# One product and one masked copy per level for both directions of a gated linear attention

## The reference

```python
def _hgrn_chunk_scan(q, k, v, log_f, s0):
    # S_t = diag(f_t) S_{t-1} + k_t outer v_t, o_t = S_t^T q_t, chunkwise
    ...
        b = jnp.cumsum(lf, axis=-2)
        diff = b[..., :, None, :] - b[..., None, :, :]
        decay = jnp.where(causal, jnp.exp(jnp.where(causal, diff, 0.0)), 0.0)
        scores = jnp.einsum('bhtd,bhtsd,bhsd->bhts', qb, decay, kb)
        o = jnp.einsum('bhts,bhsv->bhtv', scores, vb) + jnp.einsum('bhtd,bhdv->bhtv', qb * jnp.exp(b), S)
    ...

def _hgrn_bidir(q, v, lf_f, k_f, lf_b, k_b, s_f, s_b):
    o_f, s_f = _hgrn_chunk_scan(q, k_f, v, lf_f, s_f)
    rev = lambda a: jnp.flip(a, axis=1)
    o_b, s_b = _hgrn_chunk_scan(rev(q), rev(k_b), rev(v), rev(lf_b), s_b)
    return o_f + rev(o_b), s_f, s_b
```

## Time and profile before

| | us |
|---|---|
| median of 3 runs | 4889.44 |
| lowest and highest run | 4884.33, 4891.63 |
| span of the profiled execution | 4883.9 |
| TensorE busy in it | 4403.1 (90%) |
| VectorE busy | 2831.0 (58%) |
| ScalarE busy | 1812.8 (37%) |
| masked copies L1311, 120 of them | 0.735 each (median) |

### The profile page before, as it was taken

One profiled execution on the slowest core, in us unless ns is written; L12 is line 12 of the kernel. 1 busy time (PEld: TensorE's weight loads), 2 busy tenths in 40 slices (PEclk: granted clock), 3 DMA queues, 4 the chain that ended last, 5 costly groups with the idle time before them and its releaser, 6 DMA issues. The chain is left out here.

```text
span 4883.9 us, 59716 instructions
## 1 busy us (share of the span) xinstructions
PE 4403.1 (90%) x22171; PEld 3685.4 (75%) x22171; DVE 2831.0 (58%) x4958; ACT 1812.8 (37%) x2536; POOL 413.0 (8%) x308
## 2 busy tenths in 40 slices
PE   7988888878998566999999996999999999999998
PEld 5877775655874255999999995767878877777887
DVE  0777776674445987888888886334343333444332
ACT  1655654443321033333333333336233233543322
POOL 0000000000002501222222220000000000000000
PEclk9999999998999788999999998999999999999999
DMA  7111111102221025777778873211323322122332
GB/s 263 56 40 36 38 35 43 39 13 79 93 86 53 18 104 229 280 269 278 282 268 278 282 267 107 69 61 48 98 90 98 94 96 65 46 76 91 99 93 84
DMA packets 196095, 579.63 MB, mean 119 GB/s; under 512 B 17344, under 2 KB 66752, under 8 KB 194368
## 3 DMA queue, kind: packets, MB, share of 16 engines
q1 hardware_dynamic: 158032, 435.34, 26.2%
q0 software_dynamic: 36864, 134.23, 8.1%
q10 hardware_dynamic: 1008, 7.49, 0.4%
HBM read 549.73 MB, written 27.26 MB: 118 GB/s over the span
## 5 line engine op out<-in xcount | busy, mean ns | idle before, releaser
L402 DVE TENSOR_TENSOR tile_rest<-tile_raw,tile_up 128x1024 fp32r<-128x1024 f32 (+2 forms) x288 | 338.6, 1180 | 787.7 <-ACT tile_up L393 787.5
L410 PE MATMUL layer_psum<-hn_up,tile_up 128*128 128x512 f32 x1344 | 534.7, 398 | 21.2 <-DVE hn_rest L497 21.2
L411 PE MATMUL layer_psum<-hn_up,tile_rest 128*128 128x512 f32 x1344 | 527.4, 392 | 0.0
L412 PE MATMUL layer_psum<-hn_rest,tile_up 128*128 128x512 f32 x1344 | 527.2, 392 | 0.0
L393 ACT ACTIVATE tile_up<-tile_raw 128x1024 fp32r<-128x1024 f32 (+2 forms) x288 | 291.4, 1017 | 369.6 <-PE layer_psum L412 368.5
L2190 PE MATMUL ex_psum<-ex_t_up,ex_u_up 128*128 128x384 f32 x1024 | 344.0, 336 | 11.3 <-ACT ex_prod L2264 5.9
L2208 PE MATMUL ex_psum<-ex_prod_up,ex_v_up 128*128 128x384 f32 x1024 | 342.8, 335 | 2.8 <-DVE xT L2330 2.8
L2191 PE MATMUL ex_psum<-ex_t_up,ex_u_rest 128*128 128x384 f32 x1024 | 343.7, 336 | 0.0
L2192 PE MATMUL ex_psum<-ex_t_rest,ex_u_up 128*128 128x384 f32 x1024 | 343.6, 336 | 0.0
L2209 PE MATMUL ex_psum<-ex_prod_up,ex_v_rest 128*128 128x384 f32 x1024 | 342.8, 335 | 0.0
L2210 PE MATMUL ex_psum<-ex_prod_rest,ex_v_up 128*128 128x384 f32 x1024 | 342.6, 335 | 0.0
(11 more groups left out here) (448 smaller groups left out, 10119.2 us busy)
## 6 DMA issues: line engine op xcount, KB each, us to landing
ex_u<-in_peer_u SPq DMA_DIRECT2D x128, 512.0 KB, 6.8
tT<-in_peer_v SPq DMA_DIRECT2D x128, 512.0 KB, 7.3
tile_raw<-in_w_gu SPq DMA_DIRECT2D x88, 512.0 KB, 3.5
xT<-in_w_head SPq DMA_DIRECT2D x56, 512.0 KB, 3.6
mod_w<-in_w_ada SPq DMA_DIRECT2D x48, 512.0 KB, 4.8
mg_w_raw<-in_w_merge SPq DMA_DIRECT2D x48, 512.0 KB, 3.6
expert_table<-et_rows SPq DMA_DIRECT2D x6, 4096.0 KB, 11.3
ex_rows<-expert_table SPq DMA_DIRECT2D x64, 384.0 KB, 7.9
```

Of the source, the lines that this page charges most:

```text
L402: self.nc.vector.tensor_tensor(out=self.rest[:, n % self.SLOTS, 0:blocks, :], in0=self.raw[n % self.RAWS][:, 0:blocks, :], in1=self.up[:, ...
L410: self.nc.tensor.matmul(dst, w_up, up, start=first, stop=False)
L411: self.nc.tensor.matmul(dst, w_rest, up, start=False, stop=False)
L412: return self.nc.tensor.matmul(dst, w_up, rest, start=False, stop=last)
```

## The change

For levels 0 to 6 the slots are filled by role instead of by direction: `qk[slot][:, KEYS, :]` takes the scaled keys of both directions, `qk[slot][:, QUERIES, :]` the scaled queries. In each pair of blocks the left half of KEYS holds the forward keys and the right half the backward keys, and QUERIES the other way round, so that a product of a block of KEYS with the same block of QUERIES holds the wanted scores of both directions. There are 4 products a level instead of 8, one copy under one mask instead of two, and 8 masks instead of 15. The multiplications keep their number and form and write to other rows. The score banks still follow in turn, but each level takes one instead of two; the waits for `o_squared` and `o_raw` move to levels 2 and 3, those for `masked` start at level 4, and the products after level 6 use other banks. Levels 7 and 8 are computed as before.

```diff
-N_MASKS = 2 * IN_CHUNK + 1
+N_MASKS = IN_CHUNK + 1
...
+    KEYS, QUERIES = 0, 1
...
+        SCORES = IN_CHUNK + 6
...
-                n = 0
                 for level in range(IN_CHUNK):
                     pe.wait_ge(qk_ready, START + h * (LEVELS + 1) + level + 1)
-                    for dr in range(2):
-                        if n == 2:
-
-                            pe.wait_ge(o_squared, START + h)
-                        elif n == 3:
-                            pe.wait_ge(o_raw, START + h)
-                        elif n >= 4:
-                            pe.wait_ge(masked, START + h * N_MASKS + n - 3)
-                        for b in range(TB):
-                            blk = qk[qk_at(level)][:, dr, b * P:(b + 1) * P]
-                            last = nc.tensor.matmul(score_bank(n)[:, b * P:(b + 1) * P], blk, blk, start=True, stop=True)
-                        last.then_inc(score_filled, 1)
-                        n += 1
+                    if level == 2:
+
+                        pe.wait_ge(o_squared, START + h)
+                    elif level == 3:
+                        pe.wait_ge(o_raw, START + h)
+                    elif level >= 4:
+                        pe.wait_ge(masked, START + h * N_MASKS + level - 3)
+                    for b in range(TB):
+                        s = slice(b * P, (b + 1) * P)
+                        last = nc.tensor.matmul(score_bank(level)[:, s], qk[qk_at(level)][:, KEYS, s],
+                                                qk[qk_at(level)][:, QUERIES, s], start=True, stop=True)
+                    last.then_inc(score_filled, 1)
...
-                pe.wait_ge(masked, START + h * N_MASKS + n - 3)
+                pe.wait_ge(masked, START + h * N_MASKS + 4)
                 for b in range(TB):
                     s = slice(b * P, (b + 1) * P)
-                    last = nc.tensor.matmul(B[4][:, s], ksum[:, s], q[:, s], start=True, stop=True)
+                    last = nc.tensor.matmul(B[5][:, s], ksum[:, s], q[:, s], start=True, stop=True)
...
-                pe.wait_ge(masked, START + h * N_MASKS + 12)
+                pe.wait_ge(masked, START + h * N_MASKS + 5)
...
-                    last = nc.tensor.matmul(B[5][:, at * P:(at + 1) * P], qk[qk_at(7)][:, dr, s * P:(s + 1) * P],
+                    last = nc.tensor.matmul(B[6][:, at * P:(at + 1) * P], qk[qk_at(7)][:, dr, s * P:(s + 1) * P],
...
-                    dve.wait_ge(score_filled, START + h * 20 + n + 1)
+                    dve.wait_ge(score_filled, START + h * SCORES + n + 1)
...
-                    bank = score_bank(n) if n < 2 * IN_CHUNK else B[4]
+                    bank = score_bank(n)
...
-                        dve.wait_ge(score_filled, START + h * 20 + 2 * (level - QK_TURNS) + 2)
+                        dve.wait_ge(score_filled, START + h * SCORES + level - QK_TURNS + 1)
...
                         g = halves(grow[:, level % 2, dr, :], level, T)
-                        out = halves(qk[qk_at(level)][:, dr, :], level, T)
                         for side in range(2):
 
-                            by = q if side == 1 - dr else k[:, dr, 0:T]
+                            of = QUERIES if side == 1 - dr else KEYS
+                            by = q if of == QUERIES else k[:, dr, 0:T]
+                            out = halves(qk[qk_at(level)][:, of if level < IN_CHUNK else dr, :], level, T)
                             ins = nc.vector.tensor_tensor(out=out[:, :, side, :], in0=g[:, :, side, :],
                                                           in1=halves(by, level, T)[:, :, side, :], op=ALU.mult)
...
-                        to_blocks(2 * level - 2)
-                        to_blocks(2 * level - 1)
+                        to_blocks(level - 1)
...
-        masks += [same & left_s & ~left_t, same & ~left_s & left_t]
+        masks.append(same & (left_s != left_t))
```

More of the change, by code:

```diff
@@ L921, in head @@
                 pe.wait_ge(qk_ready, START + h * (LEVELS + 1) + LEVELS)
-                pe.wait_ge(masked, START + h * N_MASKS + 13)
+                pe.wait_ge(masked, START + h * N_MASKS + 6)
                 for b in range(2):
-                    last = nc.tensor.matmul(B[6][:, b * C:(b + 1) * C], qk[qk_at(8)][:, 0, b * P:(b + 1) * P],
+                    last = nc.tensor.matmul(B[7][:, b * C:(b + 1) * C], qk[qk_at(8)][:, 0, b * P:(b + 1) * P],
                                             qk[qk_at(8)][:, 0, C:T], start=True, stop=True)
                 last.then_inc(score_filled, 1)
-                pe.wait_ge(masked, START + h * N_MASKS + 14)
+                pe.wait_ge(masked, START + h * N_MASKS + 7)
                 for b in range(2):
-                    last = nc.tensor.matmul(B[7][:, b * C:(b + 1) * C], qk[qk_at(8)][:, 1, C + b * P:C + (b + 1) * P],
+                    last = nc.tensor.matmul(B[4][:, b * C:(b + 1) * C], qk[qk_at(8)][:, 1, C + b * P:C + (b + 1) * P],
                                             qk[qk_at(8)][:, 1, 0:C], start=True, stop=True)
@@ L940, in head @@
                     for dr in range(2):
-                        last = nc.tensor.matmul(B[4 + b][:], full[:, dr, T + b * P:T + (b + 1) * P], full[:, dr, 0:T],
+                        last = nc.tensor.matmul(B[5 + b][:], full[:, dr, T + b * P:T + (b + 1) * P], full[:, dr, 0:T],
                                                 start=dr == 0, stop=dr == 1)
@@ L1050, in keys @@
                     act.wait_ge(k_read, START + h)
-                    act.wait_ge(score_filled, START + (h - 1) * 20 + 15)
+                    act.wait_ge(score_filled, START + (h - 1) * SCORES + N_MASKS)
                 evacuate(("k0", h), k[:, 0, 0:T], bank_of(("k0", h)))
@@ L1136, in head @@
                     keys(h + 1)
-                act.wait_ge(score_filled, START + h * 20 + 16)
+                act.wait_ge(score_filled, START + h * SCORES + N_MASKS + 1)
                 for at, (s, t) in enumerate(((0, 1), (2, 3), (1, 0), (3, 2))):
-                    nc.scalar.activation(sx[:, s, t * P:(t + 1) * P], B[5][:, at * P:(at + 1) * P],
+                    nc.scalar.activation(sx[:, s, t * P:(t + 1) * P], B[6][:, at * P:(at + 1) * P],
                                          ACT.Copy).then_inc(score_out, 1)
@@ L1142, in head @@
                     magnitudes(h + 1)
-                act.wait_ge(score_filled, START + h * 20 + 17)
-                nc.scalar.activation(sx[:, 0:2, C:T], B[6][:].rearrange("p (b t) -> p b t", b=2),
+                act.wait_ge(score_filled, START + h * SCORES + N_MASKS + 2)
+                nc.scalar.activation(sx[:, 0:2, C:T], B[7][:].rearrange("p (b t) -> p b t", b=2),
                                      ACT.Copy).then_inc(score_out, 1)
-                act.wait_ge(score_filled, START + h * 20 + 18)
-                nc.scalar.activation(sx[:, 2:4, 0:C], B[7][:].rearrange("p (b t) -> p b t", b=2),
+                act.wait_ge(score_filled, START + h * SCORES + N_MASKS + 3)
+                nc.scalar.activation(sx[:, 2:4, 0:C], B[4][:].rearrange("p (b t) -> p b t", b=2),
                                      ACT.Copy).then_inc(score_out, 1)
@@ L1151, in head @@
                 for b in range(CB):
-                    act.wait_ge(score_filled, START + h * 20 + 19 + b)
-                    nc.scalar.activation(sc[:, b, :], B[4 + b][:], ACT.Copy).then_inc(score_out, 1)
+                    act.wait_ge(score_filled, START + h * SCORES + N_MASKS + 4 + b)
+                    nc.scalar.activation(sc[:, b, :], B[5 + b][:], ACT.Copy).then_inc(score_out, 1)
                 if more:
```

## The result

| | before | changed |
|---|---|---|
| median (us) | 4886.89 (4 runs) | 4840.32 (4 runs) |
| lowest and highest run | 4883.86, 4891.63 | 4839.83, 4842.53 |
| ratio, with its 95% interval | | 0.9905, 0.9893 to 0.9917 |
| span of the profiled execution | 4883.9 | 4840.7 |
| TensorE, VectorE, ScalarE busy | 4403.1, 2831.0, 1812.8 | 4356.1, 2788.2, 1813.2 |

The change takes 46.6 us off the median and 43.2 off the span; the forecast was 43.8, and 4845.6 as a median. The total is right. Its parts are less so: the odd heads gave more than forecast, the even heads less, and the first phase a little more.

What follows compares the result with a forecast made beforehand. TensorE's queue was taken to bind odd heads, a mixed chain of TensorE, VectorE and ScalarE even heads. Gains of 29.8 + 12.9 + 1.1 = 43.8 us from 4889.4 gave 4845.6 us, range 4834 to 4862.

Steps and rivals of the forecast that it cites:

- Odd heads bound by TensorE: Heads 0, 1, 3, 5, 7: TensorE's queue has no gap, so halved products save 5.95 us each, 29.8 us.
- half of it is 0.85 us: A level's products take 1.70 us of TensorE's queue; halving them saves 0.85 us, 5.95 us a head.
- It can hardly be more: Odd heads: the gain hardly exceeds 5.95 us each, since TensorE stays full and what follows is untouched.
- Even heads: Heads 2, 4, 6: a mixed chain of TensorE, VectorE and ScalarE gains 4.3 us each, 12.9 us; bounds 2.8 and 5.8.
- this takes TensorE's slow stretch as it is: Even heads, around level 6: the lower clock stays as before; its 1.5 us could vanish or come twice.
- rival B's first case: One more clock fall in each even head costs 4.6 us, giving 4850.2 us, inside the forecast's own range.
- Rival A: Only odd heads gain; ScalarE's table loads and cuts hold even heads: 30.9 us, 4858.5 us; chance 0.12.
- Rival B: TensorE idles more, so its clock falls more often; two more falls in all eight heads, 4870.1 us: chance 0.05.
- Rival C: Slower: clock falls reach the fills; two whole fills per head at the lower level give 4937 us; chance 0.03.
- Rival D: Nothing gained in heads, which end on ScalarE's chain; only the masks' 1.1 us remain, 4888 us; chance 0.04.
- Masks: First phase: seven masks no longer loaded shorten TensorE's wait for a weight tile by 1.1 us; bounds 0 and 1.5.
- Waits and operands: Heads: moved waits for o_squared, o_raw and free banks, and distinct operands of a product, were priced at 0.

Runs made afterwards that it cites:

- e7: Changed kernel, but the mask table keeps the room of 15 masks in SBUF, with 8 loaded and used: 4844.8 us.
- e2: Changed kernel, but each masked copy of levels 0 to 6 is issued twice: 4858.3 us.
- e4: Changed kernel, plus unused products of constants on TensorE before levels 1 and 6 in heads 2, 4 and 6: 4830.2 us, ratio to before 0.9881.
- e3: Changed kernel, but 15 masks are loaded instead of 8, the seven more unused: 4847.5 us.
- e8: Changed kernel, with the queries' fill moved behind level 5 and 10 unused products before level 1 in heads 2, 4 and 6: 4829.3 us.

## Why the prediction was right, and where its terms were off

**Odd heads bound by TensorE (29.8 us): right, and undersized.** Measured: 6.3, 6.3, 6.4, 6.0 and 6.5 us, together 31.6. The step that was mis-sized is "half of it is 0.85 us". The products' place did not halve from 1.70 to 0.85 but went to 0.81, so each level gave 0.89; it is 0.81 in e7 too, where the tiles stand as before. 7 x 0.89 = 6.2. Why half the products take less than half the place, no run shows. "It can hardly be more" was wrong by that much. That VectorE would keep up was right: its level 8 and TensorE's fill arrived together again, and e2 shows what it costs where it does not (1.8 us).

**Even heads (12.9 us): the chain was right, the size was not.** Measured: 2.7, 3.2 and 3.8 us, together 9.7, just below to inside the bounds of 2.8 and 5.8. The step that failed is "this takes TensorE's slow stretch as it is". The longer gaps brought a second fall of the clock in each even head, in the head's end (head 2) or behind level 1 (heads 4 and 6), which was rival B's first case; it should have had the larger chance, since the forecast itself said that both gaps would grow. And in head 2 the fall before level 6 reached further than before. ScalarE's start of the head and TensorE behind level 6, before:

```profile
302.86 1.49 ACT L1097 ACTIVATE hd_k<-hd_k 128x1536 f32<-128x1536 f32 x1
...
347.76 0.48 PE L601 MATMUL mx_psum<-x_up,mx_w_up 128*128 128x512 f32 x1
...
353.42 1.05 PE L917 MATMUL mx_psum<-attT 128*128 128x128 f32 x8
...
358.85 3.67 PE L941 MATMUL mx_psum<-hd_full 128*128 128x512 f32 x8 [2.64 <-DVE convT L1311]
```

And in the changed kernel (the head starts at 287.98):

```profile
328.48 0.77 PE L601 MATMUL mx_psum<-x_up,mx_w_up 128*128 128x512 f32 x1
...
334.90 1.05 PE L918 MATMUL mx_psum<-attT 128*128 128x128 f32 x8
...
340.32 5.37 PE L942 MATMUL mx_psum<-hd_full 128*128 128x512 f32 x8 [2.64 <-DVE convT L1312]
```

Up to level 6 the working came out: its products stand 37.07 us behind the head's start instead of 40.81 (343.67), 3.7 us sooner where 3.45 were worked out. From there to L918 it takes 9.85 us where it took 9.75, although one halved product had to make it 0.85 shorter: the clock was already low when the gap ended, and the fourth fill took 6.42 us instead of 5.66. The fall in the head's end then stretched L942 from 3.67 to 5.37 us, of which 0.95 came through to the next products.

e4 shows the size of the falls. Heads 4 and 6, free of them, are 6.4 and 6.9 us shorter than before; head 2, with the one in its end left, 5.2. These gains include the fall that each head had before the change, so they answer to the upper bound of 5.8 and not to the 4.3. They pass even that, since heads 4 and 6 of before were 69.3 and 69.7 us long and not 69.0 like head 2, the one that the working read.

**Rival A** fell: even heads did gain. **Rival B**'s sign was met: a clock below 1 in stretches where it was 1 before was on the prediction's own list of what would show it wrong, and here it stands in the even heads and in head 1. **Rival C** did not come: the falls lengthened one fill of an even head by up to 1.8 us (7.3 instead of 5.5). **Rival D** fell with the first head.

**Masks (1.1 us): the size fits, the cause is not settled.** The first phase's products end 1.5 us sooner, and e3 gives 1.3 for the load; but e4, with the small load, ends as late as e3, and part of the difference is a fall of the clock that the prediction did not have. The heads begin 2.2 us sooner; the 0.7 us between goes with a shorter slow stretch of the clock in the first fills (e3, which ends the phase 1.3 us later, begins its heads 1.9 us later).

**Waits and operands (0): right.** No new idle time stands before a level's products in odd heads, and L910's products kept their 0.81 us.

**What lies around the span.** "5.5 us below the median, outside the span and unchanged" was wrong. The changed kernel's profiled run has a time of 4842.53 for a span of 4840.7, 1.8 us outside; the rest of the 5.5 was spread between runs. With a fourth run the median of before is 4886.9 instead of 4889.4, which brought the forecast of the median 2.5 us too high. "Everything behind it keeps its length" came out, 4142.2 and 4142.5 us, but by luck: the stretch shown under e3 is 5.5 us shorter than before (134.2 us) and later ones make up for it, and the other kernels show that this part moves by up to 15 us.

## What to carry to other kernels

Ask which engine's queue has no gap, and price an edit by what it takes out of that queue: here half of the products was worth some 40 us and half of the copies next to nothing by itself, though in an even head both engines were busy for about as long (56.5 and 53.6 us in head 2). When an edit lengthens idle time on TensorE, count a fall of its clock as likely, and look for work to put there: moving two fills into the gaps brought 14 us more, and even products that nobody reads brought 10. Look behind the place that you filled as well: the gap of a moved fill opens where it was taken from. Judge small edits by the length of the stage that they touch, since unchanged stages moved by more than the edit was worth.

## What the runs showed that was not expected

The place of tiles in SBUF changes the pace of a fill: 5.67 and 5.57 us for 24 products of 512 columns, 5.78 and 5.83 for 48 of 256, with nothing else changed. Why is open; no run separates which tile's place does it.

The clock falls in other gaps from one profiled execution to the next, in stages that are the same: 128.7 us and 134.1 us for one stretch of the second block in two kernels that differ only in seven masks loaded at the start. Whether the small shift in time does it, or whether it differs between executions of one kernel as well, is open: no run sets the shift on purpose, each kernel has one profile, and the four timed runs of e8 alone lie between 4822.8 and 4833.3 us.
